# Projecting the retention values feature-major and turning them on TensorE, in place of a token-major projection

## The chip, the cores and the metric

The kernel runs on one core of one Trainium2 chip, in one launch. The metric is the device time of an execution in microseconds (us); the lower, the better. Of the kernel before the change three runs are known: 2089.01 us in the median, 2088.53 to 2089.17.

## The reference, cut to what matters

Two layers of a conditioned decoder trunk run over a prompt of 512 tokens and 8 samples of 8 tokens (64 sample tokens). All arrays are float32. The part that the change touches is the projection of the values `v` and what follows it in the retention:

```python
h = rmsnorm(x, norm1_g[l]) * (1.0 + sc1) + sh1
z = h @ w_in                                   # 1024 -> 8192 columns
q, k, v, g, xl, gl, ma, mb = jnp.split(z, offs, axis=-1)   # v: columns 1024 to 2047
...
scores = jnp.einsum('bhqd,bhkd->bhqk', qc, kc) * intra      # chunks of 128 tokens
o = (jnp.einsum('bhqk,bhkv->bhqv', scores, vc)
     + jnp.einsum('bhqd,bhdv->bhqv', qc, s) * q_decay[None, :, :, None])
s = (s * chunk_decay[None, :, None, None]
     + jnp.einsum('bhkd,bhkv->bhdv', kc * k_decay[None, :, :, None], vc))
```

Both sums over the tokens of a chunk need `v` with tokens on partitions, while every other part of `z` is used with features on partitions.

## The kernel before

Activations lie with features on partitions: 8 tiles of 128 features by 576 tokens, kept as two halves of 256 prompt and 32 sample tokens. Weights come in tiles of 128 x 1024 over a stream of 512 KB transfers into four slots (`raw`). ScalarE rounds each tile to `weight_h` (`split_h`, L393), VectorE takes the rest as `weight_l` (`split_l`, L749), and TensorE works with three products, high x high, high x low and low x high. Both halves of a weight tile have two buffers, so the tile after next is split while the next one is worked on.

An ordinary stage calls `stream_tile` (L1208). It makes 128 features of all 576 tokens in `acc[j % 2]`: 8 slices of the contraction, 3 products, 2 halves of 288 columns, so 48 matmuls.

The values are the exception. Their eight tiles per layer are packed token-major: each holds two slices of the contraction by 512 value columns. `v_chunk` (L1360) takes 128 tokens of `h_hi` or `h_lo` as the stationary operand and 512 value columns as the moving one, so that one of four banks of `acc` collects 128 tokens x 512 values; a tile is 4 chunks x 2 slices x 3 products = 24 matmuls. The 64 sample tokens are done apart by `v_samples` (L1369), in plain float32 from the unrounded `h_s` and `raw`, 2 matmuls a tile, which the trace shows as 4. For this the norms of the mixer write the sample columns to `h_s` (`tmp_s`, L769, L434), and a slot of `raw` is free only when the tile is done (`load_step`). After four tiles ScalarE copies the four banks to `v_tok` (L488), and VectorE adds the two halves of the samples to `v_s` (L840, L842).

Then comes the merge-gate stage, in which eight ordinary tiles alternate with the retention's chunks: scores (L1400), a transpose of the keys (L1401), the tile, four transposes of the normed output of the chunk before (`turn_o`, L1391), and the products with `v_tok` (L1413, L1416). In layer 0 a group of the modulation (L1291) and its transposes (L1302) stand behind the first and second value tile. Each engine works through its own list in the order written; semaphores hold it back.

Of the kernel before, what the change touches and what calls it, by code (L numbers as in the profile page):

```python
# [25 lines left out]
F32 = mybir.dt.float32  # L26
# [68 lines left out]


def prompt(tile):
    return tile[:, :, 0:HALF_P]
# [6 lines left out]
def build(nc, stream, ada_in, x_in, c_in, small_in, fg_in, h0_in, conv_in, wrg_in, state_in, const_in,  # L105
          y_out, ret_p_out, lru_out, conv_out, ret_s_out):
    ctx = ExitStack()
    with ctx:
# [46 lines left out]
        k_ss = place("k_ss", [128, NB_S], F32, lo + 16640)  # L155
        h_s = place("h_s", [128, KT, NB_S], F32, lo + 16384)
        on_s = place("on_s", [128, DV], F32, lo + 16896)
# [61 lines left out]
        rstd_ready, xn_ready, h_rounded, h_ready = sem("rstd_ready"), sem("xn_ready"), sem("h_rounded"), sem("h_ready")  # L219
        qk_ready, v_done, v_odd, v_ready = sem("qk_ready"), sem("v_done"), sem("v_odd"), sem("v_ready")  # L220
        ma_ready = sem("ma_ready")
# [23 lines left out]
        def carry(eng):  # L245
# [6 lines left out]
            "dve": (x_mlp, x_mixed, qk_ready, conv_kept, lru_u_ready, scans_done, y_ready, gelu_ready, s_ready),  # L252
            "act": (o_t_ready, s_o_t_ready, gates_read, state_stored[0], state_stored[1], ret_p_stored),
            "pe": (o_ready, s_o_ready),
# [6 lines left out]
        def samples(tile):  # L261

            return tile[:].rearrange("p k (a c) -> p k a c", a=2)[:, :, :, HALF_P:HALF]

        def tmp_s(n):

            return samples(tmp) if n % 2 else h_s[:].rearrange("p k (a c) -> p k a c", a=2)

# [24 lines left out]
        def _(sp):  # L293
# [21 lines left out]
            def load_step(lay, t):  # L315
                sp.wait_ge(l_split, lay * LAYER_TILES + (t + 1))
                if t >= AT_V:
                    sp.wait_ge(tile_done, lay * LAYER_TILES + (t + 1))
                load(lay * LAYER_TILES + (t + 4), t % 4)
# [6 lines left out]
            for lay in range(DEPTH):  # L326
                if lay == 0:
                    for t in range(AT_MA):
                        load_step(lay, t)
                        if t % 2 == 1 and t < 9:  # L330
                            n = ADA_PROLOGUE + t // 2
                            load_ada(n, n - 1)
                else:
                    load_range(lay, 0, AT_V)
                    for t in range(AT_V, AT_MA):
                        load_step(lay, t)
                load_range(lay, AT_MA, AT_OUT + 4 - AT_MA)
# [28 lines left out]
        def _(act):  # L366
# [60 lines left out]
            def high(n, shift_at):  # L427

                for m in range(KT):
                    act.wait_ge(xn_ready, n * 9 + (m + 2 if n and m else m + 1))  # L430
                    A(prompt(one(h_hi, m)), prompt(one(tmp, m)), ACT.Identity, bias=column(ada, m + shift_at)).then_inc(h_rounded, 1)
                    if m == 0:
                        act.wait_ge(xn_ready, n * 9 + (2 if n else 9))
                        A(samples(h_hi), tmp_s(n), ACT.Copy).then_inc(h_rounded, 1)  # L434

# [14 lines left out]
            for lay in range(DEPTH):  # L450
# [33 lines left out]
                for j in range(8):  # L484
                    if j % 4 == 3:
                        for c in range(4):
                            act.wait_ge(v_done, lay * 8 + j - 3 + c + 1)
                            A(v_tok[:, c, j // 4 * 512:j // 4 * 512 + 512], acc[c // 2][:, c % 2, :], ACT.Copy).then_inc(acc_free, 1)  # L488
                    split_h(lay, AT_V, 0, j)
                    ada_between(AT_V + j)  # L490

                def o_evac(i, c, n):
# [208 lines left out]
        def _(dve):  # L701
# [63 lines left out]

            def shift_samples(n, shift_at):

                dst = tmp_s(n).rearrange("p k a (b t) -> p k a b t", t=DS)
                V.tensor_tensor(dst, by_sample(tmp), to_samples(ada[:, shift_at:shift_at + KT, :]), ALU.add).then_inc(xn_ready, 1)  # L769

            def low(n, shift_at):

                dve.wait_ge(h_rounded, n * 9 + 2)
                V.tensor_tensor(samples(h_lo), tmp_s(n), samples(h_hi).bitcast(F32), ALU.subtract).then_inc(h_ready, 1)
                for m in range(KT):
                    dve.wait_ge(h_rounded, n * 9 + (m + 2 if m else 1))
                    V.scalar_tensor_tensor(prompt(one(h_lo, m)), prompt(one(tmp, m)), column(ada, m + shift_at), prompt(one(h_hi, m)).bitcast(F32),  # L777
                                           ALU.add, ALU.subtract).then_inc(h_ready, 1)

            def norm(n, scale, shift_at):  # L780
# [8 lines left out]
                for m in range(KT):  # L789
                    dve.wait_ge(scaled, n * KT + m + 1)  # L790
                    V.tensor_tensor(prompt(one(tmp, m)), prompt(one(tmp, m)), spread_p, ALU.mult).then_inc(xn_ready, 1)  # L791
                    if m == (0 if n else KT - 1):
                        dve.wait_ge(s_scaled, 2 * n + 2)
                        dve.wait_ge(ada_ready, NORM_SHIFT[n] + 2)
                        shift_samples(n, shift_at)
                if n % 2 == 0:
# [3 lines left out]
            for lay in range(DEPTH):  # L800
# [33 lines left out]

                for j in range(8):
                    if j % 4 == 3:
                        half = j // 4
                        v_half = v_s[0:NB_S, half * 512:half * 512 + 512]
                        done(lay, AT_V, 0, j)
                        V.tensor_copy(v_half, misc[NB_S:2 * NB_S, half, :]).then_inc(v_odd, 1)  # L840
                        dve.wait_ge(v_odd, lay * 2 + half + 1)
                        V.tensor_tensor(v_half, misc[0:NB_S, half, :], v_half, ALU.add).then_inc(v_ready, 1)  # L842
                    split_l(lay, AT_V, 0, j)

# [347 lines left out]
        def _(pe):  # L1192
# [87 lines left out]
            for lay in range(DEPTH):  # L1280
# [67 lines left out]

                def v_chunk(j, c):

                    first, last_k = j % 4 == 0, j % 4 == 3
                    cols = slice((c // 2) * HALF + (c % 2) * CHUNK, (c // 2) * HALF + (c % 2) * CHUNK + CHUNK)
                    if first:
                        pe.wait_ge(acc_free, lay * LAYER_TILES + AT_V + (c // 2 + 1 if j == 0 else c + 3))
                    for kk in range(2):
                        k = 2 * (j % 4) + kk
                        wh, wl = (w[:, j % 2, kk * 512:(kk + 1) * 512] for w in (weight_h, weight_l))
                        t_hi, t_lo = (one(t, k).rearrange("p a b -> p (a b)")[:, cols] for t in (h_hi, h_lo))
                        for n, (t, w) in enumerate(((t_hi, wh), (t_hi, wl), (t_lo, wh))):
                            last = M(acc[c // 2][:, c % 2, :], t, w, start=(first and kk == 0 and n == 0), stop=(last_k and kk == 1 and n == 2))  # L1360
                    if last_k:
                        last.then_inc(v_done, 1)
                    return last

                def v_samples(j):

                    for kk in range(2):
                        k = 2 * (j % 4) + kk
                        last = M(misc[NB_S * kk:NB_S * (kk + 1), j // 4, :], h_s[:, k, :], raw[:, j % 4, kk * 512:(kk + 1) * 512], start=(j % 4 == 0), stop=(j % 4 == 3))  # L1369
                    return last  # L1370

                for j in range(8):
                    pe.wait_ge(l_split, lay * LAYER_TILES + (AT_V + j + 1))
                    for c in range(2):
                        v_chunk(j, c)
                    if j % 4 != 3:
                        v_samples(j)
                    for c in range(2, 4):
                        last = v_chunk(j, c)
                    if j % 4 == 3:  # L1380
                        last = v_samples(j)
                    last.then_inc(tile_done, 1)
                    ada_between(AT_V + j)

                def turn_o(n):
# [8 lines left out]
                for i in range(2):  # L1394
                    for c in range(4):
                        n = lay * 8 + (i * 4 + c)
                        pe.wait_ge(stage_ready, n + 1)
                        for e in range(2):
                            qc = qk[:, bass.ds(lay * 0 + (i * 2 + e), 1), (c // 2) * HALF + (c % 2) * CHUNK:(c // 2) * HALF + (c % 2) * CHUNK + CHUNK].rearrange("p o t -> p (o t)")
                            M(misc[:, 0, e * 256:e * 256 + 128], k_st[:, c % 2, e, :], qc, start=True, stop=True)  # L1400
                            last = nc.tensor.transpose(misc[:, 0, e * 256 + 128:e * 256 + 256], k_st[:, c % 2, e, :], ident)  # L1401
                        last.then_inc(scores_ready, 1)
                        stream_tile(lay, AT_MA, lay * 0, 4 * i + c, h_hi, h_lo)
                        if i or c:
                            turn_o(lay * 8 + (i * 4 + c - 1))
                        pe.wait_ge(masked_ready, n + 1)
                        if n == lay * 8:
                            pe.wait_ge(acc_free, lay * LAYER_TILES + AT_MA + 2)
                            pe.wait_ge(v_ready, lay * 2 + 2)
                        pe.wait_ge(s_ready, n + 1)  # L1410
# [149 lines left out]

def token_major(w):

    return w.reshape(4, 2, 128, 2, 512).transpose(3, 0, 2, 1, 4).reshape(-1, 128, 1024)


def ada_tiles(w):
# [70 lines left out]
```

## Time and profile before

| quantity | value |
| --- | --- |
| median of three runs | 2089.01 us |
| the profiled execution's own time | 2088.21 us |
| its span | 2086.40 us |
| TensorE matmul busy | 2055.1 us (98%) |
| VectorE busy | 1063.9 us (51%) |
| ScalarE busy | 727.4 us (35%) |
| mean granted TensorE clock | 0.997 |

The span runs from the first to the last instruction that the profiler recorded; the execution's own time is 1.81 us longer. Busy time of TensorE counts each matmul from its start to a modelled end, and matmuls overlap, so the time that one costs in a row of its kind is read from the chain of work that ended last, which counts from end to end, or from start to start in the timeline.

### The profile page before, as it was taken

The numbers are of one execution on the slowest core, as the hardware profiler recorded it, in microseconds if no ns is written. First come the engines' busy times: TensorE is split into PE (matmuls) and PEld (weight loads), VectorE is DVE, ScalarE is ACT, GpSimd is POOL, SyncE is SP. The second block draws the span as 40 slices with busy tenths as digits, with TensorE's granted clock in tenths as the row PEclk, the third lists the DMA queues.
The fourth block names the chain that finished last, engine by engine and source line by source line (L and its number), as shares of the span: only waits on it lengthen the run. The fifth ranks groups of instructions, "written<-read, shape, count | busy, mean of one in ns | idle before, by whom it ended". The sixth has DMA issues, their size and how long they took to land.

```text
span 2086.4 us, 35707 instructions
## 1 busy us (share of the span) xinstructions
PE 2055.1 (98%) x14844; PEld 1938.5 (93%) x14844; DVE 1063.9 (51%) x1667; ACT 727.4 (35%) x915; POOL 231.2 (11%) x238
## 2 busy tenths in 40 slices
PE   6999999999999999999999999999999999999997
PEld 3869989999998999999988898999999899999996
DVE  5615566674436444444464355667634553435353
ACT  4124444665223222222231344456632321212122
POOL 0001120000041010101320011100001310101014
PEclk9999999999999999999999999999999999999998
DMA  8523242222262232323622314322222522222222
GB/s 350 182 71 107 94 158 90 79 81 81 81 243 100 85 118 82 122 81 122 230 78 68 111 57 147 124 84 82 85 80 93 212 81 82 87 85 82 81 81 102
DMA packets 78920, 232.61 MB, mean 111 GB/s; under 512 B 7360, under 2 KB 27840, under 8 KB 78528
## 3 DMA queue, kind: packets, MB, share of 16 engines
q1 hardware_dynamic: 56304, 204.86, 28.2%
q10 hardware_dynamic: 22480, 25.78, 3.8%
q8 instruction: 105, 1.72, 0.3%
q14 instruction: 31, 0.25, 0.0%
HBM read 218.52 MB, written 12.09 MB: 111 GB/s over the span
## 4 chain that ended last, share of the span: by engine, by line
PE 97%; DVE 2%; DMA 1%; ACT 0%; SPq 0%; issue 0%; DVEq 0%; POOL 0%
PE acc L1208 81%; PE acc L1360 4%; PE misc L1291 2%; PE misc L1479 1%; PE acc L1261 1%; DMA first_raw<-ada_in 1%; PE misc L1440 1%; PE misc L1369 1%; PE acc L1269 1%; PE misc L1413 1%; PE misc L1416 1%; DVE tmp L791 1%; PE misc L1302 0%; PE misc L1415 0%; DVE h_lo L777 0%; PE misc L1433 0%
## 5 line engine op out<-in xcount | busy, mean ns | idle before, releaser
L393 ACT ACTIVATE weight_h<-raw 128x1024 fp32r<-128x1024 f32 x288 | 305.1, 1060 | 1092.0 <-PE acc L1208 989.4
L1208 PE MATMUL acc<-h_hi,weight_h 128*128 128x288 f32 x2688 | 583.0, 298 | 0.0
L1208 PE MATMUL acc<-h_hi,weight_l 128*128 128x288 f32 x2688 | 575.2, 296 | 0.0
L1208 PE MATMUL acc<-h_lo,weight_h 128*128 128x288 f32 x2688 | 574.9, 295 | 0.0
L749 DVE TENSOR_TENSOR weight_l<-raw,weight_h 128x1024 fp32r<-128x1024 f32 x288 | 400.0, 1389 | 260.4 <-ACT weight_h L393 259.7
L1208 PEld LDWEIGHTS acc<-h_hi,weight_h 128*128 128x128 f32 x2688 | 433.2, 189 | 10.3 <-issue 6.5
L1208 PEld LDWEIGHTS acc<-h_lo,weight_h 128*128 128x128 f32 x2688 | 432.7, 189 | 0.0
L1208 PEld LDWEIGHTS acc<-h_hi,weight_l 128*128 128x128 f32 x2688 | 432.7, 189 | 0.0
L1208 PE MATMUL acc<-b_hi,weight_l 128*128 128x288 f32 x1536 | 328.9, 296 | 0.0
L1208 PE MATMUL acc<-b_hi,weight_h 128*128 128x288 f32 x1536 | 328.9, 296 | 0.0
L1208 PE MATMUL acc<-b_lo,weight_h 128*128 128x288 f32 x1280 | 274.1, 296 | 0.0
L1208 PEld LDWEIGHTS acc<-b_hi,weight_h 128*128 128x128 f32 x1536 | 247.6, 189 | 0.0
L1208 PEld LDWEIGHTS acc<-b_hi,weight_l 128*128 128x128 f32 x1536 | 247.6, 189 | 0.0
L1051 DVE SCALAR_TENSOR_TENSOR x<-acc,ada,x 128x512 f32 x80 | 60.1, 751 | 309.5 <-PE acc L1208 309.5
L1208 PEld LDWEIGHTS acc<-b_lo,weight_h 128*128 128x128 f32 x1280 | 206.3, 189 | 0.0
L1176 POOL TENSOR_TENSOR tmp<-tmp 128x576 f32<-128x576 f32 x64 | 73.5, 1148 | 659.9 <-DVE tmp L1073 659.9
L1073 DVE TENSOR_SCALAR tmp<-acc 128x576 f32<-128x576 f32 x64 | 48.5, 758 | 178.7 <-PE acc L1208 176.4
L1106 POOL TENSOR_TENSOR qk<-x 128x576 f32<-128x576 f32 x4 | 8.2, 2062 | 557.9 <-DVE x L1056 557.9
L665 ACT ACTIVATE b_hi<-tmp 128x576 fp32r<-128x576 f32 x64 | 43.9, 687 | 59.0 <-POOL tmp L1176 59.0
L1108 POOL TENSOR_TENSOR qk<-x 128x576 f32<-128x576 f32 x24 | 48.2, 2008 | 75.2 <-DVE x L1056 75.2
L1208 PE MATMUL acc<-o_lo,weight_h 128*128 128x288 f32 x256 | 54.8, 296 | 0.0
L1360 PE MATMUL acc<-weight_h,h_hi 128*128 128x512 f32 x128 | 52.1, 407 | 0.0
(209 smaller groups left out, 1860.3 us busy)
## 6 DMA issues: line engine op xcount, KB each, us to landing
raw<-stream SPq DMA_DIRECT2D x290, 512.0 KB, 3.5
ada_raw<-ada_in SPq DMA_DIRECT2D x48, 512.0 KB, 6.2
first_raw<-ada_in SPq DMA_DIRECT2D x36, 512.0 KB, 14.7
s_s<-state_in ACTq DMA_DIRECT2D x8, 1024.0 KB, 6.9
ret_s_out<-s_s ACTq DMA_DIRECT2D x8, 1024.0 KB, 4.5
two_raw<-ada_in SPq DMA_DIRECT2D x12, 512.0 KB, 11.3
x<-x_in ACTq DMA_DIRECT2D x1, 2304.0 KB, 13.3
wrg<-wrg_in ACTq DMA_DIRECT2D x18, 128.0 KB, 3.0
```

What stands on the lines that cost most here:

```text
L393: A(weight_h[:, j % 2, :], raw[:, (j + 2) % 4, :], ACT.Copy).then_inc(h_split, 1)
L665: A(one(b_hi, m), tmp[:, 2 + m % 2, :].rearrange("p (a b) -> p a b", a=2), ACT.Copy).then_inc(u_rounded, 1)
L749: V.tensor_tensor(weight_l[:, j % 2, :], raw[:, (j + 2) % 4, :], weight_h[:, j % 2, :].bitcast(F32), ALU.subtract).then_inc(l_split, 1)
L791: V.tensor_tensor(prompt(one(tmp, m)), prompt(one(tmp, m)), spread_p, ALU.mult).then_inc(xn_ready, 1)
L1051: V.scalar_tensor_tensor(prompt(one(x, m)), prompt(a), gate, prompt(one(x, m)), ALU.mult, ALU.add)
L1073: V.tensor_scalar(tmp[:, j % 2, :].rearrange("p (a b) -> p a b", a=2), acc[j % 2][:, :, 0:HALF], 0.0, None, ALU.max).then_inc(acc_free, 1)
L1108: G.tensor_tensor(qk[:, 1, :], x[:, m, :], x[:, m, :], ALU.mult).then_inc(square_chain, 1)
L1176: G.tensor_tensor(tmp[:, 2 + j % 2, :], tmp[:, j % 2, :], tmp[:, j % 2, :], ALU.mult).then_inc(u_ready, 1)
L1208: last = M(acc[j % 2][:, half, 0:HALF], w, r[:, k, half * HALF:(half + 1) * HALF], start=(k == 0 and n == 0), stop=(k == KT - 1 and n == 2))
L1261: M(acc[j][:, half, 0:HALF], w[:, j, k * 128:(k + 1) * 128], h_hi[:, k, half * HALF:(half + 1) * HALF], start=(k == 0 and w is weight_h), ...
L1291: last = M(misc[cols, 2 + p % 2, :], c_act[:, k, at_col:at_col + COLS], slots[j][:, kk * 512:(kk + 1) * 512], start=(odd == 0 and k < 4), ...
L1360: last = M(acc[c // 2][:, c % 2, :], t, w, start=(first and kk == 0 and n == 0), stop=(last_k and kk == 1 and n == 2))
```

## The change

The values become ordinary tiles. Their weights are packed as all others are, `stream_tile` makes them with features on partitions for prompt and samples together, VectorE copies each finished tile to `o_t` (two instructions, which free `acc`), and one tile later TensorE turns it with five transposes: four of 128 tokens, one of the 64 sample tokens. ScalarE copies the turned tile to `v_tok` and `v_s`. `h_s`, the samples' own matmuls, VectorE's two instructions per half and the wait of the weight loads for a finished tile go.

```diff
@@ SyncE: the loads of the value tiles
-                if t >= AT_V:
-                    sp.wait_ge(tile_done, lay * LAYER_TILES + (t + 1))
@@ ScalarE
                 for j in range(8):
-                    if j % 4 == 3:
-                        for c in range(4):
-                            act.wait_ge(v_done, lay * 8 + j - 3 + c + 1)
-                            A(v_tok[:, c, j // 4 * 512:j // 4 * 512 + 512], acc[c // 2][:, c % 2, :], ACT.Copy).then_inc(acc_free, 1)
                     split_h(lay, AT_V, 0, j)
                     ada_between(AT_V + j)
+                    act.wait_ge(v_turned, lay * 8 + j + 1)
+                    A(v_tok[:, :, j * 128:(j + 1) * 128], misc[:, v_bank(j), :].rearrange("p (c d) -> p c d", c=4), ACT.Copy)
+                    A(v_s[0:NB_S, j * 128:(j + 1) * 128], misc[0:NB_S, v_bank(j) + 1, 0:128], ACT.Copy).then_inc(v_ready, 1)
@@ VectorE
-                        V.tensor_copy(v_half, misc[NB_S:2 * NB_S, half, :]).then_inc(v_odd, 1)
-                        V.tensor_tensor(v_half, misc[0:NB_S, half, :], v_half, ALU.add).then_inc(v_ready, 1)
+                with dve.Fori(0, 2) as i:
+                    for j in range(4):
+                        done(lay, AT_V, i, j)
+                        dst = o_t[:, 2 + j % 2, :]
+                        V.tensor_copy(dst[:, 0:SEQ].rearrange("p (a b) -> p a b", a=2), prompt(acc[j % 2]))
+                        V.tensor_copy(dst[:, SEQ:TOK].rearrange("p (a b) -> p a b", a=2), sample(acc[j % 2])).then_inc(acc_free, 1)
+                        split_l(lay, AT_V, i, j)
@@ TensorE
+                def turn_v(n, j):
+                    pe.wait_ge(acc_free, n[0] + (j + 3))
+                    pe.wait_ge(v_ready, n[1] + j + 1)
+                    src = o_t[:, 2 + j % 2, :]
+                    bank = v_bank(j)
+                    for c in range(4):
+                        nc.tensor.transpose(misc[:, bank, c * 128:(c + 1) * 128], src[:, c * 128:(c + 1) * 128], ident)
+                    nc.tensor.transpose(misc[0:NB_S, bank + 1, 0:128], src[:, SEQ:TOK], ident).then_inc(v_turned, 1)
                 for j in range(8):
-                    ... (v_chunk and v_samples)
+                    stream_tile(lay, AT_V, 0, j, h_hi, h_lo)
+                    if j:
+                        turn_v(n, j - 1)
                     ada_between(AT_V + j)
@@ TensorE, in the first chunk of the retention, between its scores and its tile
+                        if n == lay * 8:
+                            turn_v(v_base, 7)
```

`v_bank(j)` is 2 for the last two tiles and 0 for the others: the turned tile lies in two banks of `misc`, 0 and 1 or 2 and 3. `v_ready` starts at 1, so the wait in `turn_v` for tile j asks that tile j - 1 has been copied out.

On TensorE, inside the value stage of layer 1, before (L1360 is a value matmul, L1369 the samples):

```order
L1360 MATMUL acc<-weight_h,h_hi 128x512
L1360 MATMUL acc<-weight_l,h_hi 128x512
L1360 MATMUL acc<-weight_h,h_lo 128x512
L1369 MATMUL misc<-raw,h_s 64x512 x2
L1360 MATMUL acc<-weight_h,h_hi 128x512
```

and now, between two value tiles (L1200 is `stream_tile`, L1348 and L1349 the five transposes):

```order
L1200 MATMUL acc<-h_lo,weight_h 128x288 x2
L1200 MATMUL acc<-h_hi,weight_l 128x288 x2
L1348 MATMUL misc<-const,o_t 128x128 [waits v_ready,acc_free]
L1348 MATMUL misc<-const,o_t 128x128 x3
L1349 MATMUL misc<-const,o_t 64x128
L1200 MATMUL acc<-h_hi,weight_h 128x288 [waits acc_free,l_split]
```

The matmuls over 512 columns and the samples' block are gone; a tile has 48 matmuls over 288 columns, and five transposes with two waits follow.

On TensorE, where the value stage of layer 1 meets the first chunk of the retention, before (L1400 and L1401 are scores and the keys' transpose):

```order
L1360 MATMUL acc<-weight_h,h_lo 128x512
L1369 MATMUL misc<-raw,h_s 64x512 x2
L1400 MATMUL misc<-qk,k_st 128x128 [waits stage_ready]
L1401 MATMUL misc<-const,k_st 128x128
L1208 MATMUL acc<-h_hi,weight_h 128x288 [waits acc_free,l_split]
```

with one more pair of L1400 and L1401 ahead of L1208; and now (L1374 and L1375 are the same two):

```order
L1348 MATMUL misc<-const,o_t 128x128 x3
L1349 MATMUL misc<-const,o_t 64x128
L1374 MATMUL misc<-qk,k_st 128x128 [waits stage_ready]
L1375 MATMUL misc<-const,k_st 128x128
L1374 MATMUL misc<-qk,k_st 128x128
L1375 MATMUL misc<-const,k_st 128x128
L1348 MATMUL misc<-const,o_t 128x128 [waits v_ready,acc_free]
L1348 MATMUL misc<-const,o_t 128x128 x3
```

The last two turns stand only the scores apart, and the second waits for the copy of the first.

On ScalarE, at the end of the value stage of layer 1, before (L393 is `split_h`, L488 the copy to `v_tok`):

```order
L393 ACTIVATE weight_h<-raw 128x1024 [waits raw_loaded0,tile_done]
L488 ACTIVATE v_tok<-acc 128x512 [waits v_done] x4
L393 ACTIVATE weight_h<-raw 128x1024 [waits raw_loaded1,tile_done]
L506 DMA s_s<-state_in 128x8x256 [waits state_stored0]
L393 ACTIVATE weight_h<-raw 128x1024 [waits raw_loaded2,tile_done]
```

and now (L389 is `split_h`, L484 and L485 the copies of a turned tile):

```order
L389 ACTIVATE weight_h<-raw 128x1024 [waits raw_loaded0,tile_done]
L484 ACTIVATE v_tok<-misc 128x4x128 [waits v_turned]
L485 ACTIVATE v_s<-misc 64x128
L389 ACTIVATE weight_h<-raw 128x1024 [waits raw_loaded1,tile_done]
L484 ACTIVATE v_tok<-misc 128x4x128 [waits v_turned]
L485 ACTIVATE v_s<-misc 64x128
L501 DMA s_s<-state_in 128x8x256 [waits state_stored0]
```

Each rounding of weights but the stage's first now stands behind a copy that waits for TensorE's turn.

## Rows read from the trace of the kernel before

**Rows 1.** The page: busy time by engine; the chain's shares by line.

```profile
PE 2055.1 (98%) x14844; PEld 1938.5 (93%) x14844; DVE 1063.9 (51%) x1667; ACT 727.4 (35%) x915; POOL 231.2 (11%) x238
...
PE acc L1208 81%; PE acc L1360 4%; PE misc L1291 2%; PE misc L1479 1%; PE acc L1261 1%; DMA first_raw<-ada_in 1%; PE misc L1440 1%; PE misc L1369 1%; PE acc L1269 1%; PE misc L1413 1%; PE misc L1416 1%; DVE tmp L791 1%; PE misc L1302 0%; PE misc L1415 0%; DVE h_lo L777 0%; PE misc L1433 0%
```

**Rows 2.** Busy time by stretch: window, length, each engine (instructions), clock, DMA.

```profile
1122.50:1176.55 54.05, 54.05 (x227) 37.02 (x226) 14.02 (x14) 13.28 (x16) 2.68 (x8) 1.00 0.20 69
...
157.50:235.70 78.20, 78.20 (x548) 75.58 (x546) 44.72 (x113) 38.35 (x45) 9.16 (x27) 1.00 0.25 85
41.20:45.00 3.80, 3.80 (x19) 3.80 (x18) 3.80 (x7) 2.97 (x5) 0.00 (x0) 0.55 1.03 402
```

**Rows 3.** Chain, value stage of layer 1: start, time added, what, instructions.

```profile
1122.66 2.74 PE acc L1360 x12
1125.41 1.01 PE misc L1369 x4
1126.41 5.74 PE acc L1360 x24
...
1175.50 1.01 PE misc L1369 x4
1176.51 0.42 PE misc L1400 x2
1176.93 0.11 PE misc L1401
1177.04 0.22 PE misc L1400 x2
...
1177.37 6.38 PE acc L1208 x48
```

**Rows 4.** Chain, transposes in both layers' retention.

```profile
1186.14 6.39 PE acc L1208 x48
1192.53 0.44 PE misc L1391 x4
...
253.14 0.37 PE misc L1465 x2
253.51 0.26 PE misc L1421 x2
253.77 0.23 PE misc L1422
254.00 6.38 PE acc L1208 x48
```

**Rows 5.** Instructions of L1391: duration ns, least, median, most.

```profile
L1391 PE MATMUL misc<-const,on_p x64: 270/272/273, 172.7 to 1262.2; 128*128 128x128 f32 x64
```

**Rows 6.** Timeline and groups: a turn, ScalarE's copies and rounding.

```profile
182.80 0.60 PE L1391 MATMUL misc<-const,on_p 128*128 128x128 f32 x4
...
183.44 0.60 ACT L496 ACTIVATE o_t<-misc 128x512 f32<-128x512 f32 x1 [4.93 <-PE misc L1391]
183.93 1.05 ACT L393 ACTIVATE weight_h<-raw 128x1024 fp32r<-128x1024 f32 x1
...
L555 ACT ACTIVATE o_t<-misc 128x64 f32<-128x64 f32 x16 | 2.6, 221 | 0.0
```

**Rows 7.** Timeline, VectorE: behind a finished tile, `split_l`, copies.

```profile
100.11 0.76 DVE L828 SCALAR_TENSOR_TENSOR o_t<-acc,const 128x576 f32<-128x576 f32 x1 [4.22 <-PE acc L1208]
...
102.43 1.23 DVE L749 TENSOR_TENSOR weight_l<-raw,weight_h 128x1024 fp32r<-128x1024 f32 x1
...
166.38 0.68 DVE L860 COPY s_p<-misc 128x512 f32<-128x512 f32 x1
...
1060.83 0.21 DVE L1053 TENSOR_TENSOR x_part<-acc,ada 128x64 f32<-128x64 f32 x1
```

**Rows 8.** Instructions of L434: duration with `h_s` and without.

```profile
L434 ACT ACTIVATE h_hi<-h_s x2: 615/622/629, 39.2 to 1069.1; 128x512 fp32r<-128x512 f32 x2
L434 ACT ACTIVATE h_hi<-tmp x2: 631/632/632, 637.3 to 1657.5; 128x512 fp32r<-128x512 f32 x2
```

More of the change, by code:

```diff
@@ L94, in one, with v_bank @@
     return buf[:, bass.ds(m, 1), :].rearrange("p o (a b) -> p (o a) b", a=2)
+def v_bank(j):
+    return 2 if j >= 6 else 0
 def prompt(tile):
@@ L155, in build @@
         k_ss = place("k_ss", [128, NB_S], F32, lo + 16640)
-        h_s = place("h_s", [128, KT, NB_S], F32, lo + 16384)
         on_s = place("on_s", [128, DV], F32, lo + 16896)
@@ L219, in build @@
         rstd_ready, xn_ready, h_rounded, h_ready = sem("rstd_ready"), sem("xn_ready"), sem("h_rounded"), sem("h_ready")
-        qk_ready, v_done, v_odd, v_ready = sem("qk_ready"), sem("v_done"), sem("v_odd"), sem("v_ready")
+        qk_ready, v_turned, v_ready = sem("qk_ready"), sem("v_turned"), sem("v_ready")
         ma_ready = sem("ma_ready")
@@ L252, in build @@
             "dve": (x_mlp, x_mixed, qk_ready, conv_kept, lru_u_ready, scans_done, y_ready, gelu_ready, s_ready),
-            "act": (o_t_ready, s_o_t_ready, gates_read, state_stored[0], state_stored[1], ret_p_stored),
+            "act": (v_ready, o_t_ready, s_o_t_ready, gates_read, state_stored[0], state_stored[1], ret_p_stored),
             "pe": (o_ready, s_o_ready),
@@ L263, in samples @@
             return tile[:].rearrange("p k (a c) -> p k a c", a=2)[:, :, :, HALF_P:HALF]
-        def tmp_s(n):
-            return samples(tmp) if n % 2 else h_s[:].rearrange("p k (a c) -> p k a c", a=2)
         def by_sample(tile):
@@ L333, in _ @@
                 else:
-                    load_range(lay, 0, AT_V)
-                    for t in range(AT_V, AT_MA):
-                        load_step(lay, t)
+                    load_range(lay, 0, AT_MA)
                 load_range(lay, AT_MA, AT_OUT + 4 - AT_MA)
@@ L433, in high @@
                         act.wait_ge(xn_ready, n * 9 + (2 if n else 9))
-                        A(samples(h_hi), tmp_s(n), ACT.Copy).then_inc(h_rounded, 1)
+                        A(samples(h_hi), samples(tmp), ACT.Copy).then_inc(h_rounded, 1)
             def joint(n, scale, shift_at):
@@ L764, in scale_samples, with shift_samples @@
                 V.tensor_tensor(by_sample(tmp), by_sample(source), to_samples(scale), ALU.mult).then_inc(s_scaled, 1)
-            def shift_samples(n, shift_at):
-                dst = tmp_s(n).rearrange("p k a (b t) -> p k a b t", t=DS)
-                V.tensor_tensor(dst, by_sample(tmp), to_samples(ada[:, shift_at:shift_at + KT, :]), ALU.add).then_inc(xn_ready, 1)
+            def shift_samples(shift_at):
+                V.tensor_tensor(by_sample(tmp), by_sample(tmp), to_samples(ada[:, shift_at:shift_at + KT, :]), ALU.add).then_inc(xn_ready, 1)
             def low(n, shift_at):
                 dve.wait_ge(h_rounded, n * 9 + 2)
-                V.tensor_tensor(samples(h_lo), tmp_s(n), samples(h_hi).bitcast(F32), ALU.subtract).then_inc(h_ready, 1)
+                V.tensor_tensor(samples(h_lo), samples(tmp), samples(h_hi).bitcast(F32), ALU.subtract).then_inc(h_ready, 1)
                 for m in range(KT):
@@ L794, in norm @@
                         dve.wait_ge(ada_ready, NORM_SHIFT[n] + 2)
-                        shift_samples(n, shift_at)
+                        shift_samples(shift_at)
                 if n % 2 == 0:
@@ L833, in _ @@
                         V.tensor_tensor(qk[:, off - AT_Q + j, :], o_t[:, c0, :], o_t[:, c0 + 1, :], ALU.add).then_inc(qk_ready, 1)
[L835 to L839, printed above, removed]
-                        V.tensor_copy(v_half, misc[NB_S:2 * NB_S, half, :]).then_inc(v_odd, 1)
-                        dve.wait_ge(v_odd, lay * 2 + half + 1)
-                        V.tensor_tensor(v_half, misc[0:NB_S, half, :], v_half, ALU.add).then_inc(v_ready, 1)
-                    split_l(lay, AT_V, 0, j)
+                with dve.Fori(0, 2) as i:
[5 more added lines that the diff above has]
+                        split_l(lay, AT_V, i, j)
                 for i in range(2):
@@ L1347, in _ @@
                     ada_between(t)
[L1349 to L1370, printed above, removed]
-                for j in range(8):
[L1373 to L1382, printed above, removed]
+                def turn_v(n, j):
[6 more added lines that the diff above has]
+                    nc.tensor.transpose(misc[0:NB_S, bank + 1, 0:128], src[:, SEQ:TOK], ident).then_inc(v_turned, 1)
@@ L1383, in _ @@
+                n = (lay * LAYER_TILES + AT_V, lay * 8)
+                for j in range(8):
+                    stream_tile(lay, AT_V, 0, j, h_hi, h_lo)
+                    if j:
+                        turn_v(n, j - 1)
                     ada_between(AT_V + j)
+                v_base = n
                 def turn_o(n):
@@ L1407, in _ @@
                         if n == lay * 8:
-                            pe.wait_ge(acc_free, lay * LAYER_TILES + AT_MA + 2)
-                            pe.wait_ge(v_ready, lay * 2 + 2)
+                            pe.wait_ge(v_ready, lay * 8 + 8 + 1)
+                            carry(pe)
                         pe.wait_ge(s_ready, n + 1)
@@ L1558, in tiles @@
     return w.reshape(KT, 128, -1, 128).transpose(2, 1, 0, 3).reshape(-1, 128, 1024)
-def token_major(w):
-    return w.reshape(4, 2, 128, 2, 512).transpose(3, 0, 2, 1, 4).reshape(-1, 128, 1024)
 def ada_tiles(w):
@@ L1590 @@
         cut = lambda lo, hi: tiles(z[:, lo:hi])
-        w += [cut(0, 1024), token_major(z[:, 1024:2048]), cut(5120, 6144), cut(2048, 3072), cut(3072, 4096), np.stack([cut(4096, 5120), tiles(a["w_proj_ret"][l])], axis=1).reshape(-1, 128, 1024),
+        w += [cut(0, 2048), cut(5120, 6144), cut(2048, 3072), cut(3072, 4096), np.stack([cut(4096, 5120), tiles(a["w_proj_ret"][l])], axis=1).reshape(-1, 128, 1024),
               cut(6144, 7168), tiles(a["w_proj_lru"][l]), tiles(a["w_out"][l])]
```

## The prediction

> **What bounds the kernel.** I read the page's busy times and the chain's shares first [rows 1]: TensorE is busy for 98% of the span, and the ordinary tiles of L1208 alone make 81% of the chain; the value matmuls (L1360) make 4% and their samples (L1369) 1%. Then the windows: in layer 1's value stage TensorE is busy for all 54.05 us of 54.05, VectorE and ScalarE for 14.02 and 13.28 [rows 2]. So nothing waits there for weights or evacuations, and a change of this stage is worth what it adds to or takes from TensorE's own list. That is read from the chain, which gives each block the time that it adds [rows 3, 4]; durations of single matmuls would count their overlaps twice. A window over the merge-gate stage shows the granted clock at 1.00, so at 2.4 GHz, as in the value stage [rows 2].
>
> **What goes.** The value stage of layer 1 runs from 1122.66 to 1176.51 us in the chain, 53.85 us. The first pair of scores behind it takes 0.42 where the second takes 0.22 [rows 3]; this 0.20 belongs to the sample block ahead of it, which loads 64 columns where the scores load 128. So the stage costs 54.05 us, 6.76 a tile: 24 matmuls, 5.74 behind a sample block, and 1.01 for the block. Layer 0 has the same work with one modulation group and its transposes between, which stay.
>
> **What comes, on TensorE.**
>
> 1. Eight ordinary tiles. One adds 6.38 us [rows 3, 4], so 8 x 6.38 = 51.04. The rows are those of the very function that the values now use, with the same operands.
>
> 2. Eight turns of five transposes. The row for the first four is `turn_o`: four float32 transposes of 128 columns against the identity add 0.44 [rows 4], 0.11 each, behind an ordinary tile as here. For the fifth, of 64 sample columns, the nearest row is L1422, the transpose of the samples' keys: 0.23, with an ordinary tile right behind it that takes 6.38 and so pays no return [rows 4]. Together 0.67 a turn, 5.36 for eight. From below: the fifth costs 0.11 as the others, 0.55 a turn. From above: the entry costs what it does at L1465, where two transposes take 0.37 and not 0.22, and the fifth costs the 0.26 with which the samples' scores (L1421) change from 128 to 64 columns: 0.44 + 0.15 + 0.26 = 0.85. I take 0.67, whose two rows are of the same operation and the same neighbours; the upper end comes from places that follow narrower blocks.
>
> 3. A new wait at the end of the stage. The last two turns stand only the scores apart and write the same banks of `misc`, so the second waits until ScalarE has copied the first. Let the last value tile end at 0. The first of these turns and the scores (0.22 + 0.11, twice) let TensorE reach the last turn at 0.67 + 0.66 = 1.33. In the rows of `turn_o` ScalarE starts 0.64 after the first of four transposes (182.80 to 183.44) [rows 6]; the fifth adds 0.23, so it starts at 0.87 and ends the copies, 0.60 and 0.22 [rows 6], at 1.69. That is 0.36 late. A restarted transpose must also fill the array: it lasts 0.27 from start to end [rows 5] but adds 0.11 in a row of its kind, so up to 0.16 more. The next row of ScalarE's list starts 0.11 before the copy ahead of it ends (183.93 against 184.04), which gives some back. I take 0.45, with 0.2 and 0.7 as bounds. VectorE isn't what is late here: it starts 0.2 behind a tile, and its copies take 0.68 and some 0.21 [rows 7], done at 1.1. Queued behind the waiting transpose is the first merge-gate tile, so the wait stays on the path.
>
> Sum for a layer: 51.04 + 5.36 + 0.45 = 56.85, against 54.05: 2.80 us longer, 5.6 for both. Bounds: 51.04 + 8 x 0.55 + 0.2 = 55.64 gives 1.59, 3.2 for both; 51.04 + 8 x 0.85 + 0.7 = 58.54 gives 4.49, 9.0 for both.
>
> **What is hidden.** VectorE gains two copies a tile, 0.9 us in a tile of 7; its list in the stage is idle for three quarters [rows 2]. ScalarE's copies rise from 8 x 0.60 to 8 x 0.82, but they also stand ahead of the weight rounding now: each `split_h` waits behind a copy that waits for a turn one tile later. From a tile's end: copy from 0.87 to 1.69, rounding 1.05, the rest on VectorE 1.23 [rows 6, 7], so done near 4.0. The weights are for the tile after next, which starts at 0.67 + 6.38 = 7.05, so 3 us cover it. Were they gone, each microsecond of lateness would cost one per tile, up to 16 in all. The masks of the first chunk stand behind the same split on VectorE and are wanted only behind the first merge-gate tile. The loads of the value tiles lose a wait; as TensorE never waited for weights there, nothing is gained. Without `h_s` the norms of the mixer round the samples in 0.632 and not 0.622 us [rows 8]: 0.01 twice, left out.
>
> **A rule weighed.** Transposes of `turn_o`'s shape add 0.11 each [rows 4]. The Trainium skill (TensorE: Matmul & The Clock Gate, section Back-to-back issue gap) puts a sustained pair of weight load and matmul with 128 columns at about 81 ns. By that rule, as an estimate, a turn would take 0.41, a layer 54.7, and the change would cost 1.4 us. The trace does not agree for float32 transposes: 0.44 for four, not 0.32.
>
> **Rivals.**
>
> A. Turns are paid by streamed columns, and the change is not slower. An ordinary matmul of 288 columns adds 6.38 / 48 = 0.133; 128 columns would be 0.059 by that, a turn 0.30, a layer 51.04 + 2.36 + 0.45 = 53.85: 0.4 us faster for both layers. It decides from a turn below (54.05 - 51.04 - 0.45) / 8 = 0.32. For it: an ordinary tile with all 64 samples is indeed shorter than a value tile was, 6.38 to 6.76. Against it: no transpose in the trace comes below 0.11. Between 0.32 and 0.55 the result is also no measurable change. 9%, with 2% of it for clearly faster.
>
> B. The clock falls. From 41.20 to 45.00 us the granted clock was 0.55, nearly all at the lower level, 1.2 GHz [rows 2]. If the transposes and the stall brought one such stretch to each layer, 3.80 x 0.45 = 1.7 us twice, the change would cost 9.0. Against it: 78 us with seven turns of four transposes and smaller work between tiles held 1.00 [rows 2]. The same page (section Part 4: PE-mode transpose) says that the full clock does not engage for transposes; between tiles the trace does not show this. 4%.
>
> C. The turns don't overlap. If each transpose added its whole 0.27 [rows 5], a turn would take 1.36, a layer 62.4, and the change would cost 16.7. Four in 0.44 speak against it. 2%.
>
> D. ScalarE's rounding becomes the bound, as priced above: 3 us of cover would have to go. If one tile in each layer came 2 us late, the change would cost 9.6. 3%.
>
> **The numbers.** The profiled execution took 2088.21 us, 0.80 below the median of the runs, 2089.01; 1.81 of it lies outside the span and doesn't change. 2088.21 + 5.6 = 2093.8, and brought to the median of the runs 2094.6. Its own bounds are 2092.2 and 2098.0. My forecast holds 82%. The range that leaves out 2 in 10 goes from 2091.8 to 2098.3: B and D lie at its upper edge, and A and C outside. What a measurement of this kernel can tell from no change is about 0.2%, 4.2 us, so slower counts from 2093.2. Of the forecast's 82% I put 68 above that (a turn of 0.58 or more) and 14 below; with B, C and D slower has 77%, with A within 0.2% has 21%, faster 2%.
>
> **What would show it.** In the changed profile an ordinary tile in the value stage adds 6.38 in the chain, four transposes 0.44, the fifth about 0.23, and the stage from the first value matmul to the first merge-gate one is some 2.8 us longer. TensorE has one short idle of about half a microsecond in each layer, ahead of the last turn, released by ScalarE's copy, and none ahead of a value tile. A fifth transpose at 0.11 or 0.4 moves the sum to its bounds. The forecast is wrong if TensorE waits for weights in the stage, if the granted clock there is below 1.00, or if a turn takes less than 0.5.

## The result, and the profile after

| quantity | before | after |
| --- | --- | --- |
| median (14 runs each) | 2089.09 us | 2092.93 us |
| lowest to highest | 2088.53 to 2091.19 | 2092.26 to 2095.06 |
| profiled execution, its span | 2088.21, 2086.40 us | 2092.77, 2090.90 us |
| TensorE matmuls recorded | 14844 | 15244 |

The change costs 3.84 us in the median: 1.0019 times the time before, with a 95% interval from 1.0012 to 1.0026. Forecast were 5.6 us, with 3.2 and 9.0 as the bounds of the working. The direction came out, and so did each block of the working but one, which was taken too dear.

The window over layer 1's value stage of the changed kernel, from its first value tile to the first merge-gate tile (columns as in [rows 2]):

```profile
1125.17:1181.78 56.61, 56.34 (x432) 56.13 (x432) 19.33 (x28) 13.97 (x23) 2.66 (x8) 1.00 0.24 76
```

TensorE is idle for 0.27 us in it, and the granted clock is 1.00. The stretch holds the scores of the first chunk too. In the chain of before the same stretch goes from 1122.66 to 1177.37 [rows 3], 54.71 us; now it is 56.61, which is 1.90 longer. In layer 0 the ordinary tile ahead of the value stage and the first merge-gate tile begin in the chains here, the first two lines before and the last two now:

```profile
93.48 6.58 PE acc L1208 x48
157.73 6.38 PE acc L1208 x48
93.56 12.98 PE acc L1200 x96
159.68 6.38 PE acc L1200 x48
```

The merge-gate tile begins 1.95 later, of which 0.08 was there before the stage, so the stage gained 1.87. Both layers together make 3.77, nearly the whole of the 3.84 between the medians.

The chain of the changed kernel in that stretch (start, time added, what, instructions; 336 matmuls are seven tiles, five of queries and keys and the first two of values):

```profile
1093.16 44.81 PE acc L1200 x336
1137.96 0.44 PE misc L1348 x4
1138.40 0.11 PE misc L1349
1138.51 6.39 PE acc L1200 x48
...
1173.18 6.39 PE acc L1200 x48
1179.57 0.44 PE misc L1348 x4
1180.00 0.12 PE misc L1349
1180.12 0.02 issue
1180.15 0.03 ACT v_tok L484
1180.17 0.47 issue
1180.64 0.27 ACT v_s L485
1180.91 0.14 issue
1181.04 0.63 PE misc L1348 x4
1181.67 0.11 PE misc L1349
1181.78 6.38 PE acc L1200 x48
```

A value tile adds 6.39, four transposes 0.44, both as the rows before had it [rows 3, 4]. The fifth adds 0.11, not 0.23, and the tile behind it takes no more than any other. A turn is thus 0.55. Behind the last tile the chain leaves TensorE for ScalarE's two copies and comes back for the last turn: from 1180.12 to 1181.78 there are 1.66 us, of which the scores need 0.66 and the turn 0.55, so 0.45 is the stall.

The timeline of the same place (start, length, engine; an idle time and its releaser in brackets):

```profile
1179.60 0.69 DVE L833 COPY o_t<-acc 128x512 f32<-128x512 f32 x1 [3.43 <-PE acc L1200]
...
1180.15 0.60 ACT L484 ACTIVATE v_tok<-misc 128x512 f32<-128x512 f32 x1 [5.23 <-PE misc L1349]
...
1180.21 0.21 DVE L834 COPY o_t<-acc 128x64 f32<-128x64 f32 x1
...
1180.50 0.27 PE L1375 MATMUL misc<-const,k_st 128*128 128x128 f32 x1
1180.64 0.26 ACT L485 ACTIVATE v_s<-misc 64x128 f32<-64x128 f32 x1
...
1181.01 0.42 PEld L1348 LDWEIGHTS misc<-const,o_t 128*128 128x128 f32 x4 [0.47 <-issue]
1181.04 0.63 PE L1348 MATMUL misc<-const,o_t 128*128 128x128 f32 x4 [0.27 <-ACT v_s L485]
```

The last score has started at 1180.50; ScalarE's second copy ends at 1180.90, and only then can the transposes' operand be loaded, at 1181.01. VectorE's copies are over at 1180.42, before they are wanted. Had nothing been waited for, the next transpose would have started 0.11 behind that score, at 1180.61. So the copies are 0.29 late; from their end to the first transpose it takes another 0.14, and the four transposes last 0.63 and not 0.60 [rows 6], which makes the 0.45 but for rounding. The idle time in brackets is 0.27 and not 0.45, because the modelled end of the last score covers the rest.

### The profile page after: what moved, and what is told of

Same layout as the page of the kernel before. It is cut to its first block, busy times and chain, and to the rows that moved or that the text cites. A ratio compares the mean times of both kernels' runs of the same rounds, so it can differ in the third digit from the quotient of the medians.

```text
span 2090.9 us, 36618 instructions
## 1 busy us (share of the span) xinstructions
PE 2058.0 (98%) x15244; PEld 1976.3 (95%) x15244; DVE 1071.9 (51%) x1691; ACT 728.4 (35%) x931; POOL 231.1 (11%) x238
## 4 chain that ended last, share of the span: by engine, by line
PE 97%; DVE 2%; DMA 1%; ACT 0%; issue 0%; SPq 0%; DVEq 0%; POOL 0%
PE acc L1200 86%; PE misc L1283 2%; PE misc L1455 1%; PE acc L1253 1%; DMA first_raw<-ada_in 1%; PE misc L1416 1%; PE acc L1261 1%; PE misc L1389 1%; PE misc L1392 1%; DVE tmp L785 1%; PE misc L1294 0%; PE misc L1391 0%; DVE h_lo L771 0%; PE misc L1409 0%; PE misc L1348 0%; PE misc L1365 0%
## 5 line engine op out<-in xcount | busy, mean ns | idle before, releaser
L389 ACT ACTIVATE weight_h<-raw 128x1024 fp32r<-128x1024 f32 x288 | 305.2, 1060 | 1030.1 <-PE acc L1200 999.3
L1200 PE MATMUL acc<-h_hi,weight_h 128*128 128x288 f32 x2944 | 639.0, 299 | 0.0
L1200 PE MATMUL acc<-h_hi,weight_l 128*128 128x288 f32 x2944 | 630.4, 296 | 0.0
L1200 PE MATMUL acc<-h_lo,weight_h 128*128 128x288 f32 x2944 | 629.7, 296 | 0.0
L1200 PEld LDWEIGHTS acc<-h_hi,weight_h 128*128 128x128 f32 x2944 | 474.3, 189 | 11.0 <-issue 7.4
L1200 PEld LDWEIGHTS acc<-h_lo,weight_h 128*128 128x128 f32 x2944 | 474.0, 189 | 0.0
L1200 PEld LDWEIGHTS acc<-h_hi,weight_l 128*128 128x128 f32 x2944 | 474.0, 189 | 0.0
L1200 PE MATMUL acc<-b_hi,weight_l 128*128 128x288 f32 x1536 | 329.0, 296 | 0.0
L1200 PE MATMUL acc<-b_hi,weight_h 128*128 128x288 f32 x1536 | 328.9, 296 | 0.0
L1200 PE MATMUL acc<-b_lo,weight_h 128*128 128x288 f32 x1280 | 273.9, 296 | 0.0
L1200 PEld LDWEIGHTS acc<-b_hi,weight_h 128*128 128x128 f32 x1536 | 247.6, 189 | 0.0
L1200 PEld LDWEIGHTS acc<-b_hi,weight_l 128*128 128x128 f32 x1536 | 247.6, 189 | 0.0
L1200 PEld LDWEIGHTS acc<-b_lo,weight_h 128*128 128x128 f32 x1280 | 206.3, 189 | 0.0
L1200 PE MATMUL acc<-o_lo,weight_h 128*128 128x288 f32 x256 | 54.8, 296 | 0.0
L1068 DVE TENSOR_TENSOR b_lo<-tmp,b_hi 128x576 f32 x64 | 48.2, 754 | 0.4 <-ACT b_hi L660 0.4
```

The lines of the kernel that those rows point to most:

```text
L389: A(weight_h[:, j % 2, :], raw[:, (j + 2) % 4, :], ACT.Copy).then_inc(h_split, 1)
L1068: V.tensor_tensor(one(b_lo, m), tmp[:, 2 + j % 2, :].rearrange("p (a b) -> p a b", a=2), one(b_hi, m).bitcast(F32), ALU.subtract).then_inc ...
L1200: last = M(acc[j % 2][:, half, 0:HALF], w, r[:, k, half * HALF:(half + 1) * HALF], start=(k == 0 and n == 0), stop=(k == KT - 1 and n == 2))
```

## The experiments

**The turns left out (e1).**

```diff
-                    act.wait_ge(v_turned, lay * 8 + j + 1)
-                    A(v_tok[:, :, j * 128:(j + 1) * 128], misc[:, v_bank(j), :] ...)
-                    A(v_s[0:NB_S, j * 128:(j + 1) * 128], misc[0:NB_S, v_bank(j) + 1, 0:128], ACT.Copy)
-                        V.tensor_copy(dst[:, 0:SEQ] ..., prompt(acc[j % 2]))
-                        V.tensor_copy(dst[:, SEQ:TOK] ..., sample(acc[j % 2])).then_inc(acc_free, 1)
+                        V.tensor_copy(v_tok[:, :, at_v] ..., prompt(acc[j % 2]) ...)
+                        V.tensor_copy(v_s[0:NB_S, at_v], acc[j % 2][0:NB_S, 0, 0:128]).then_inc(acc_free, 1)
-                        turn_v(n, j - 1)
-                            turn_v(v_base, 7)
...
```

> The changed kernel without its turns: the five transposes per value tile and ScalarE's copies are left out, VectorE copies each finished tile straight to the place of the turned one, so the retention works on values that were not turned. Theory (the change's time is eight ordinary tiles, eight turns of 0.55 us and a stall of 0.45 in each layer, in place of 54.05): 16 x 0.55 + 2 x 0.45 = 9.7 us go, about 2083.2, 5.8 below the kernel before; an ordinary tile still adds 6.39 in the chain. Rival (the turns lie in gaps and the ordinary tiles or something outside the stage carry the loss): within 2 us of the changed kernel, 2091 to 2093.

Measured: 2083.51 us (seven runs, 2080.40 to 2084.65), 0.9969 times the kernel before (0.9957 to 0.9980). The theory's 2083.2 holds; the rival is out by 8 us. The chain has 624 matmuls of `stream_tile` (L1197), thirteen tiles of 6.40, and then the scores (L1369) and the keys' transpose (L1370):

```profile
1088.96 83.22 PE acc L1197 x624
1172.18 0.22 PE misc L1369 x2
1172.40 0.11 PE misc L1370
```

So ordinary value tiles by themselves would be faster than the token-major stage. The turns and their stall take that back, and more.

**The last turn inside the first merge-gate tile (e2).**

```diff
-                        if n == lay * 8:
-                            turn_v(v_base, 7)
-                        stream_tile(lay, AT_MA, lay * 0, 4 * i + c, h_hi, h_lo)
+                        inside = (lambda k: turn_v(v_base, 7) if k == 4 else None) if n == lay * 8 else None
+                        stream_tile(lay, AT_MA, lay * 0, 4 * i + c, h_hi, h_lo, inside)
```

> The last turn of each layer stands in the middle of the first merge-gate tile, not ahead of it. Theory (the wait for ScalarE's copy is on the path, 0.45 us a layer): TensorE's idle time ahead of the last turn goes, about 0.9 us less than the changed kernel, 2092.0, and no new wait. Rival (the wait only moves to the products with the values behind that tile, which need the last copy): no change, 2092.9, with the idle time ahead of those products.

Measured: 2091.69 us, 1.0013 times the kernel before (1.0003 to 1.0022). By the medians that is 1.2 below the changed kernel; the intervals of the two overlap, so the trace decides. Its chain has no piece off TensorE there (L1388 is a product with the values):

```profile
1179.98 3.18 PE acc L1200 x24
1183.16 0.44 PE misc L1348 x4
1183.60 0.11 PE misc L1349
1183.71 3.19 PE acc L1200 x24
1186.90 0.43 PE misc L1388 x2
```

From the last value tile's end at 1178.77 to 1186.90 all of TensorE's time is work, and the products with the values follow the tile at once. That is 8.13 us, where the changed kernel takes 8.59 (1179.57 to 1188.16), 0.46 more. The stall was on the path and does not move on.

**The last turn but one inside the last value tile (e4).**

```diff
+                    inside = (lambda k: turn_v(n, 6) if k == 4 else None) if j == 7 else None
-                    stream_tile(lay, AT_V, 0, j, h_hi, h_lo)
-                    if j:
+                    stream_tile(lay, AT_V, 0, j, h_hi, h_lo, inside)
+                    if j and j < 7:
```

> The turn of the last tile but one stands inside the last value tile, so ScalarE's copy is done early, and the last turn stays behind the scores. Theory (VectorE's copy of the last tile is the next to be late: it is done 1.1 us behind the tile, the scores end at 0.66): the wait stays, about 0.4 us, now released by VectorE; 2092.8. Rival (ScalarE's copy alone holds the last turn): no wait, 0.9 us less, 2092.0.

Measured once: 2092.35 us, which does not tell 2092.8 from 2092.0. The chain does, and shows who is late now (L833 and L834 are VectorE's two copies to `o_t`):

```profile
1176.58 3.20 PE acc L1200 x24
1179.78 0.02 issue
1179.81 0.06 DVE o_t L833
1179.86 0.55 issue
1180.41 0.23 DVE o_t L834
1180.64 0.04 issue
1180.68 0.66 PE misc L1348 x4
```

From the end of the last tile at 1179.78 the last turn ends at 1181.45, 1.67 later, against 1.66 behind the last turn but one in the changed kernel. With ScalarE's copy out of the way VectorE's is late: in the timeline its second copy is done 1.01 us after the first score starts (1179.61 to 1180.62), near the 1.1 that the prediction had, and the scores need 0.66. One early copy is worth nothing here; only work between tile and turn covers both.

**The samples' keys turned first (e7)**, to find why the row taken for the fifth transpose was too dear.

```diff
-                    M(misc[0:NB_S, 0, 0:NB_S], k_ss[:], sample(one(qk, h)), start=True, stop=True)
-                    nc.tensor.transpose(misc[0:NB_S, 0, 128:256], k_ss[:], ident).then_inc(s_scores_ready, 1)
+                    nc.tensor.transpose(misc[0:NB_S, 0, 128:256], k_ss[:], ident)
+                    M(misc[0:NB_S, 0, 0:NB_S], k_ss[:], sample(one(qk, h)), start=True, stop=True).then_inc(s_scores_ready, 1)
```

> The kernel before, with the transpose of the samples' keys (L1422 there, 0.23 in the chain) ahead of the samples' scores (L1421, two passes, 0.26) and not behind them. Theory (the 0.23 that I took for the fifth transpose belongs to its place behind the scores' short passes, whose end comes early): ahead of them the transpose adds 0.11 to 0.14, and the scores take over the rest, 0.49 together. Rival (a transpose of 64 columns costs 0.23 wherever it stands): 0.23 here too. The time is that of the kernel before, 2089.

Measured once: 2090.47 us, inside the spread of the kernel before. Of this kernel's chain (L1421 is now the transpose, L1422 the scores, L1465 two transposes ahead of both):

```profile
254.25 0.37 PE misc L1465 x2
254.62 0.11 PE misc L1421
254.73 0.26 PE misc L1422 x2
254.99 6.59 PE acc L1208 x48
```

The transpose costs 0.11 ahead of the scores, and now the tile behind the scores pays 0.2 that it did not pay in [rows 4]. So the 0.23 was a transpose of 0.11 and part of the return from the scores' passes ahead of it. Theory and rival are told apart. The expected sum of 0.49 for the two did not hold: they are 0.37, and 0.57 with what the tile pays, against 0.49 before.

**The samples' matmuls over 128 loaded columns (e3)**, in the kernel before.

```diff
-                        last = M(misc[NB_S * kk:NB_S * (kk + 1), j // 4, :], h_s[:, k, :], raw[...], ...)
+                        last = M(misc[:, j // 4 * 2 + kk, :], h_s[:, k - kk:k - kk + 2, :]..., raw[...], ...)
...
```

> The kernel before, with 128 columns loaded for the samples' matmuls in place of 64 (the samples of two neighbouring slices side by side; the half that doesn't belong to the slice lands in rows that nobody reads), in two banks per half. Theory (the block costs 1.26 us a tile, 6.75 less 24 x 0.229, because changing between 128 and 64 loaded columns empties the array on both sides): four passes at some 0.23 remain, 0.92, so 0.34 x 16 = 5.4 us go, about 2083.6, and a value tile takes 6.4. Rival (the dear part is the float32 pass itself, or the change between the number formats): no change, 2089.

Measured: 2097.79 us, 1.0044 times the kernel before (1.0027 to 1.0061). The theory is false: instead of 5.4 us less it is 8.9 us more than before in the same series (2088.88).

```profile
1128.35 2.74 PE acc L1360 x12
1131.10 1.72 PE misc L1369 x4
1132.81 5.57 PE acc L1360 x24
...
1186.61 0.22 PE misc L1400 x2
```

What I said of the change between widths holds, as the 24 matmuls behind a block take 5.57 and not 5.74 and the scores 0.22 and not 0.42 [rows 3]. But a pass now adds 0.43, and four of them 1.72 where the block had 1.01. The block before was cheap for a reason that I had not seen.

**Both of the samples' matmuls on the same 64 columns (e6).**

```diff
-                        last = M(misc[NB_S * kk:NB_S * (kk + 1), j // 4, :], h_s[:, k, :], raw[...], ...)
+                        last = M(misc[0:NB_S, j // 4 * 2 + kk, :], h_s[:, k, :], raw[...], ...)
...
```

> The kernel before, with the samples' two matmuls of a tile both on the first 64 columns of the array (into two banks) in place of the two halves. Theory (a plain float32 pass over 512 columns takes 0.43, and the block before is cheap because its two matmuls run side by side in the two halves): four passes in a row, 1.7 us a block in place of 1.01, so 16 x 0.7 = 11 us more, about 2100. Rival (64 loaded columns alone make a pass short): 1.01 a block, 2089.

Measured once: 2101.55 us, 12 above before.

```profile
1129.79 2.74 PE acc L1360 x12
1132.53 1.86 PE misc L1369 x4
1134.39 5.70 PE acc L1360 x24
```

The second matmul moves to the other matmul's half of the array, and with it to a bank of its own, as in e3; the block grows from 1.01 to 1.86. Whether the bank has a part in that, no run tells apart. That the two matmuls overlapped before is in the timelines: in the first half-microsecond of a block two passes start in the kernel before (first line, 1125.30 to 1125.80) and one here (second line, 1132.40 to 1132.90):

```profile
1125.34 0.65 PE L1369 MATMUL misc<-raw,h_s 128*64 128x512 f32 x2
1132.46 0.64 PE L1369 MATMUL misc<-raw,h_s 128*64 128x512 f32 x1
```

So the two matmuls of the kernel before ran side by side in the two halves. On one half a pass takes 0.465 (1.86 for four, the changes of width within), near the 0.43 of e3.

**The samples in the rounded format, high and low side by side (e5).** The rival of e3's theory pointed here: not the loaded width but the plain float32 pass is dear.

```diff
-        h_s = place("h_s", [128, KT, NB_S], F32, lo + 16384)
+        h_s = place("h_s", [128, KT, 2 * NB_S], F32R, lo + 14336)
-                        last = M(misc[NB_S * kk:NB_S * (kk + 1), j // 4, :], h_s[:, k, :], raw[...], ...)
+                        for n, w in enumerate((weight_h, weight_l)):
+                            last = M(misc[:, j // 4, :], h_s[:, k, :], w[:, j % 2, kk * 512:(kk + 1) * 512], ...)
+                        if off == AT_Q and j == 1:
+                            for q, part in enumerate((h_hi, h_lo)):
+                                last = V.tensor_copy(h_s[:, :, NB_S * q:NB_S * (q + 1)]..., samples(part))
...
```

> The kernel before, with the samples of a value tile in the same rounded format as the prompt: VectorE lays the high and the low halves of the 64 sample tokens side by side once per layer (two copies in the query tiles), 128 columns are loaded, and the high and the low weights are moved past them, so 2 matmuls per slice give all four products and the existing sum of the two row halves adds them. Theory (a matmul of 512 columns in this format adds 0.229 us, a plain float32 pass over 128 loaded columns 0.43): a value tile is 28 x 0.229 = 6.40 us with no change of the loaded width, 0.35 below the kernel before, 5.7 us for 16 tiles: 2083.3. Rival (128 loaded columns make each pass of the samples 0.43, whatever the format): 2098, as the wide float32 samples.

Measured: 2084.58 us, 0.9976 times the kernel before (0.9967 to 0.9986), with 2089.43 for before in the same series. It beats both kernels: 4.9 us below the one before, and some 8 below the changed one, which ran in another series. In the chain L1364 is a value matmul, L1374 the samples, L1406 the scores:

```profile
1121.19 2.74 PE acc L1364 x12
1123.93 0.91 PE misc L1374 x4
1124.85 5.55 PE acc L1364 x24
...
1172.88 0.22 PE misc L1406 x2
```

A block of four passes adds 0.91, and nothing is paid for a change of width. The stage takes 51.69 us against 54.05, twice 2.36: 4.7. Of the 0.29 a tile, 0.10 comes from the block (1.01 to 0.91) and 0.19 from the 24 matmuls behind it (5.74 to 5.55), which no longer pay for 64 loaded columns. The expected 5.7 was too much by 0.06 a tile, mostly as the 24 matmuls take 5.55 behind a block and not 24 x 0.229 = 5.50.

## Why the prediction was right, point by point

- The view: the stage is TensorE's own list, and the chain gives its price. Shown: what the stage gained in the two layers (1.90 and 1.87) is nearly the whole difference of the medians. The two profiled executions are 4.50 apart by their spans. Another 0.5 us of that lies between 464 and 628 us, in ordinary tiles that the change does not touch: the profile before has 205 of their matmuls from 486.3 to 512.7 us, where as long a stretch of the changed kernel (466.0 to 492.4) has 201. The profiles of e3 and e6 have 204 in such a stretch too, but from 1516.0 and 1520.0 us on, so it is not the work of the value stage; its cause stays open.
- What goes, 54.05 a layer: right as a sum. That 0.20 of it is paid by the scores for the block ahead of them is shown by e3 and e5, where they take 0.22 at once. That the block loads 64 columns was only half of the reason: behind 64-column transposes nothing is paid, nor behind plain float32 matmuls with 128 loaded columns (e3).
- Eight tiles of 6.38: 6.39 in the trace, and e1 gives 2083.51 for the kernel with the tiles alone.
- Eight turns of 0.67: this is the step that failed in size, by the price of the fifth transpose, 0.23. The turns take 0.55, the lower bound, as the fifth transpose costs 0.11 like the others. 16 x 0.12 = 1.9 us is what the forecast had too much: 5.6 - 1.9 = 3.7, against 3.84 measured. The row that I took, L1422, stands behind a plain float32 matmul of 64 loaded columns and pays part of the return from it; e7 moved it and got 0.11. Its neighbours were not the same as I had written.
- The stall of 0.45, by ScalarE's copy: 0.45, by ScalarE's copy, and near the parts that I gave: the copies are 0.29 late (0.36, less what the two overlap), and the restart costs 0.17 (up to 0.16). That VectorE is not late but close shows in e4, and that the wait is on the path in e2.
- What was hidden stayed hidden: no wait of TensorE for weights in the stage, though every rounding but the stage's first stands behind a copy, and the granted clock at 1.00, though eight turns stand in the stage.
- The rivals: A needs a turn below 0.32, and no transpose came below 0.11. B, C and D have no trace in the profile. The estimate from the 81 ns a pair of the Trainium skill (TensorE: Matmul & The Clock Gate, section Back-to-back issue gap), a turn of 0.41, was 0.14 too low.
- The chances: the time rose by 0.18 to 0.19%, just under the 0.2% from which slower counts, in the part of the forecast to which I gave 14%. By that mark the call of slower, with its 77%, did not come, although the interval, 1.0012 to 1.0026, shows that the change costs time. A turn of 0.55 and not 0.58 decided it.

## What to carry to other kernels

A layout that makes an operation cheaper is paid for where it is turned back: here ordinary tiles save 5.9 us (16 times 54.05 / 8 less 6.39) and the turns with their stalls cost 9.7. Price a block by end-to-end rows of the same operation behind the same kind of instruction; the cost of a change shows in whichever instruction comes next, and a row taken behind other neighbours carries it along. And before a side computation is moved into the main stream, ask what makes it dear: four rounded matmuls over 128 loaded columns (0.91) were shorter than the four plain float32 passes over 64 (1.01), the matmuls around them no longer paid for the change, and no turn was needed at all.

## What the runs showed of the hardware that was not expected

- A plain float32 pass over 512 columns adds 0.43 us with 128 loaded columns (e3: 1.72 for four), and 0.465 with 64 on one half of the array (e6: 1.86 for four, the changes of width within), where a matmul of 512 columns in the rounded format adds 0.23 (2.74 for twelve).
- Two such matmuls with 64 loaded columns each, on different halves of the array, run side by side: 1.01 for four passes in the kernel before against 1.86 on one half (e6).
- After plain float32 matmuls with 64 loaded columns the next full-width work loses 0.2 us (scores 0.42 and not 0.22; in e7 a tile 6.59 and not 6.38); after a transpose with 64 loaded columns it loses nothing (0.11, then a tile of 6.39). Rounded matmuls with 64 loaded columns were not looked at.
